# Fourier mixing: channel frequencies 0 to 128 computed, the others written as the same tiles at mirrored tokens

## The reference, cut to what matters

```python
FNET_GROUPS, FNET_GROUP_DIM = 4, 256
def fourier_mix(h, w_o, b_o):
    hg = h.astype(jnp.float32).reshape(bsz, t, FNET_GROUPS, FNET_GROUP_DIM)
    f = jnp.fft.fft2(hg, axes=(1, 3), norm='ortho').real
    return f.reshape(bsz, t, D_MODEL).astype(h.dtype) @ w_o + b_o

hx = rmsnorm(x, norm_g[i, 0]) * (1.0 + sc1x) + sh1x
x = x + g1x * fourier_mix(hx, fnet_wo[fi], fnet_bo[fi])
```

## Time and profile before

| | us |
|---|---|
| median of 3 runs | 4153.48 |
| lowest and highest | 4148.98, 4155.55 |
| the profiled execution's own time | 4151.23 |
| its span | 4149.3 |
| its mean granted TensorE clock | 0.956 |
| TensorE busy (share of the span) | 3711.9 (89%) |
| VectorE busy | 1350.4 (33%) |
| ScalarE busy | 1014.9 (24%) |

### The profile page before, as it was taken

The page is one execution under the profiler, slowest core; times in us unless marked ns, Lnnn a source line. Parts: engine busy times, 40 slices in busy tenths (PEclk is TensorE's granted clock), DMA queues, the critical chain, the costliest instruction groups (busy, mean ns, idle before and its releaser), DMA issues.

```text
span 4149.3 us, 63323 instructions
## 1 busy us (share of the span) xinstructions
PE 3711.9 (89%) x28370; PEld 2288.8 (55%) x28370; DVE 1350.4 (33%) x2376; ACT 1014.9 (24%) x1973; POOL 264.1 (6%) x240
## 2 busy tenths in 40 slices
PE   7998999999698969999768887779989998998998
PEld 3556443434355658888443332235548884656886
DVE  2123000000545047777430000025433332534243
ACT  3012111111232135554210000113323221423231
POOL 0000000000000034434100000000000000000000
PEclk9997999999888989999979999989999999999999
DMA  8345889896034154331519999911122322112230
GB/s 288 102 148 198 304 310 363 307 341 244 33 116 162 42 114 89 69 87 42 174 41 360 375 376 387 384 54 58 51 71 92 92 88 66 55 45 88 91 99 23
DMA packets 530414, 666.74 MB, mean 161 GB/s; under 512 B 156552, under 2 KB 299144, under 8 KB 530144
## 3 DMA queue, kind: packets, MB, share of 16 engines
q1 hardware_dynamic: 506352, 627.37, 44.6%
q10 hardware_dynamic: 19952, 22.81, 1.7%
q0 software_dynamic: 3840, 12.52, 0.8%
HBM read 631.18 MB, written 31.46 MB: 160 GB/s over the span
## 4 chain that ended last, share of the span: by engine, by line
PE 72%; DVE 10%; DMA 6%; SPq 4%; ACT 4%; POOL 2%; ACTq 1%; issue 1%; DVEq 0%; POOLq 0%
PE ps L620 11%; DMA ring<-in_moe_wu 5%; PE ps L625 4%; SPq L2652 4%; PE ps L483 3%; PE ps L813 3%; PE ps L2515 3%; PE ps L2516 3%; PE ps L2517 3%; PE ps L2531 3%; PE ps L2532 3%; PE ps L2530 3%; PE ps L786 3%; PE ps L2151 3%; PE ps L2257 3%; POOL ring L1323 2%
## 5 line engine op out<-in xcount | busy, mean ns | idle before, releaser
L620 PE MATMUL ps<-ring,H 128*64 128x512 f32 x2048 | 494.4, 602 | 52.4 <-DMA ring<-in_moe_wu 39.2
L620 PEld LDWEIGHTS ps<-ring,H 128*64 128x64 f32 x2048 | 146.9, 137 | 343.7 <-issue 253.9
L722 DVE TENSOR_TENSOR scr<-ps,scr 128x512 f32<-128x512 f32 x32 | 22.1, 691 | 965.2 <-PE ps L625 516.9
L620 PE MATMUL ps<-ring,scr 128*64 128x512 f32 x1024 | 248.3, 599 | 39.9 <-DMA ring<-in_moe_wd 38.5
L2515 PE MATMUL ps<-scr_rounded,ring_rounded 128*128 128x512 f32 x512 | 205.0, 400 | 23.0 <-ACT scr_rounded L2553 23.0
L2584 DVE TENSOR_TENSOR ring_rounded<-ring,scr_rounded 128x2048 fp32r<-128x2048 f32 x64 | 146.7, 2292 | 227.6 <-ACT scr_rounded L2550 227.6
L2516 PE MATMUL ps<-H_rounded,scr_rounded 128*128 128x512 f32 x512 | 204.8, 400 | 0.0
L2517 PE MATMUL ps<-scr_rounded 128*128 128x512 f32 x512 | 204.5, 399 | 0.0
L2532 PE MATMUL ps<-scr_rounded 128*128 128x512 f32 x512 | 202.6, 396 | 0.0
L2530 PE MATMUL ps<-scr_rounded,ring_rounded 128*128 128x512 f32 x512 | 202.0, 394 | 0.0
L2550 ACT ACTIVATE scr_rounded<-ring 128x2048 fp32r<-128x2048 f32 x64 | 122.1, 1908 | 257.7 <-PE ps L2532 246.4
(11 more groups left out here) (405 smaller groups left out, 6246.1 us busy)
## 6 DMA issues: line engine op xcount, KB each, us to landing
ring<-in_moe_wg SPq DMA_DIRECT2D x128, 1024.0 KB, 9.2
ring<-in_moe_wu SPq DMA_DIRECT2D x128, 1024.0 KB, 8.4
ring<-in_moe_wd SPq DMA_DIRECT2D x128, 1024.0 KB, 11.3
ring<-in_mlp_w SPq DMA_DIRECT2D x64, 1024.0 KB, 5.5
ring<-in_ada_w SPq DMA_DIRECT2D x48, 1024.0 KB, 8.0
ring<-in_w_in SPq DMA_DIRECT2D x14, 1024.0 KB, 5.2
ring<-in_w_out SPq DMA_DIRECT2D x8, 1024.0 KB, 5.2
st_kka<-scr ACTq DMA_DIRECT2D x16, 384.0 KB, 3.5
```

What stands on the lines that cost most here:

```text
L620: ins = pe.matmul(bx[64 * n:64 * n + 64, :], stat_x(k), w[:, k % 4, :], start=k == 0, stop=k == KT - 1)
```

## The change

The first table has 256 columns in place of 512: 129 cosines (frequencies 0 to 128) and 127 sines (frequencies 1 to 127). Two groups share a PSUM bank in the first transform. After it, VectorE and ScalarE put the columns of a bank in two places: in Z, frequencies 0 to 127 of the cosine and, from column 129 on, 1 to 127 of the sine (column 128, the sine of frequency 0, is set to zero once); and in ZH, a new tile, the cosine of frequency 128, one column per group at columns 0, 32, 64 and 96, the rest being zero.

The second transform makes one new tile per sequence from ZH (`fh`) and then, for each group, one tile of frequencies 0 to 127 instead of two tiles. Each such tile is written to H twice: as it is to tile 2g, and with its token columns reversed to tile 2g+1 (token 0 apart, by a copy of its own). Partition 0 of tile 2g+1, where frequency 128 belongs, is then overwritten from the `fh` tile. ScalarE takes groups 1 and 3, VectorE 0 and 2. The rows of the output weights are put in the matching order on the host. The modulation blocks in the first transform stand after the 1st, 2nd, 4th, 5th, 7th, 8th, 10th and 11th of its 12 banks; in the second, one after each group's tile.

```diff
-        DFT_C = S(12288, 2, 512)
+        DFT_C = S(12288, 2, 256)
...
-        Z = S(0, 6, 4, 512)
+        Z = S(0, 6, 4, 256)
+        ZH = S(6144, 6, P)
+        YH = [S(6912, TX), S(6912 + TX, TC)]
...
         def fnet_tensor(pe):
...
             for tt in range(6):
+                for gg in range(2):
+                    b = bank(pe, f"f1.{tt}.{gg}")
+                    for g in (2 * gg, 2 * gg + 1):
+                        o = 256 * (g % 2)
+                        for k in range(2):
...
+                            ins = pe.matmul(b[:, o:o + 256], H[:, 2 * g + k, tt * P:tt * P + P], DFT_C[:, k, :], start=k == 0, stop=k == 1)
+                    did(T_, ins.then_inc(tensor_done, 1), f"f1.{tt}.{gg}")
+                    if (2 * tt + gg) % 3 < 2:
+                        ada_tensor(pe, ADA_F1[0] + (2 * tt + gg) // 3 * 2 + (2 * tt + gg) % 3)
+            for s0, sn, tts in ((TX, TC, (4, 5)), (0, TX, (0, 1, 2, 3))):
...
+                for tt in tts:
+                    for gg in range(2):
+                        if later(pe, f"free.f1.{tt}.{gg}"):
+                            pe.wait_ge(*at(f"free.f1.{tt}.{gg}"))
+                b = bank(pe, f"fh.{s0}")
+                for n, tt in enumerate(tts):
+                    ins = pe.matmul(b[:, 0:sn], ZH[:, tt, :], table_of(n, 0), start=n == 0, stop=n == len(tts) - 1)
+                did(T_, ins.then_inc(tensor_done, 1), f"fh.{s0}")
                 for g in range(4):
...
+                    b = bank(pe, f"f2.{g}.{s0}")
                     for cs in range(2):
                         for n, tt in enumerate(tts):
...
+                            ins = pe.matmul(b[:, 0:sn], Z[:, tt, g, cs * P:cs * P + P], table_of(n, cs),
                                             start=cs == 0 and n == 0, stop=cs == 1 and n == len(tts) - 1)
...
+                    ada_tensor(pe, ADA_F2[0] + (0 if s0 else 4) + g)
+            linear_tensor(pe, "fo", "fwo", lambda k, s0, sn: H[:, k, s0:s0 + sn], SEGS, lambda k: f"fy.{k}",
                           between=lambda n: ada_tensor(pe, ADA_FO[0] + n))
...
         def fnet_scalar(act):
+            if later(act, "fz"):
+                act.wait_ge(*at("fz"))
             for tt in range(6):
+                for gg in range(2):
+                    if gg:
+                        t = tile(act, f"f1.{tt}.{gg}").rearrange("p (g c) -> p g c", c=256)
+                        for lo, hi in ((0, P), (P + 1, 2 * P)):
+                            did(A_, act.activation(Z[:, tt, 2:4, lo:hi], t[:, :, lo:hi], ACT.Copy).then_inc(scalar_done, 1))
+                        did(A_, act.activation(ZH[:, tt, 64:P].rearrange("p (g c) -> p g c", c=32)[:, :, 0:1], t[:, :, P:P + 1],
+                                               ACT.Copy).then_inc(scalar_done, 1), f"free.f1.{tt}.{gg}")
...
+            for s0, sn in (SEGS[1], SEGS[0]):
+                y = YH[1 if s0 else 0]
+                t = tile(act, f"fh.{s0}")
+                did(A_, act.activation(y, t[:, 0:sn], ACT.Copy).then_inc(scalar_done, 1), f"free.fh.{s0}")
                 for g in range(4):
                     if g % 2:
+                        t = tile(act, f"f2.{g}.{s0}")
+                        did(A_, act.activation(H[:, 2 * g + 1, s0 + 1:s0 + sn], t[:, sn - 1:0:-1], ACT.Copy).then_inc(scalar_done, 1))
+                        did(A_, act.activation(H[:, 2 * g + 1, s0:s0 + 1], t[:, 0:1], ACT.Copy).then_inc(scalar_done, 1))
+                        did(A_, act.activation(H[:, 2 * g, s0:s0 + sn], t[:, 0:sn], ACT.Copy).then_inc(scalar_done, 1), f"free.f2.{g}.{s0}")
+                        act.wait_ge(*own(act, A_))
+                        did(A_, act.activation(H[0:1, 2 * g + 1, s0:s0 + sn], y[32 * g:32 * g + 1, :], ACT.Copy).then_inc(scalar_done, 1))
...
+                    ada_scalar(act, ADA_F2[0] + (0 if s0 else 4) + g)
...
         def fnet_vector(dve):
+            did(V, dve.memset(Z[:, :, :, P:P + 1].rearrange("p t g c -> p (t g) c"), 0.0).then_inc(vector_done, 1))
+            did(V, dve.memset(ZH[:, :, :], 0.0).then_inc(vector_done, 1), "fz")
+            dve.wait_ge(*own(dve, V))
...
-    c["dftC"] = np.concatenate([cs, sn], 1)
+    c["dftC"] = np.concatenate([cs[:, 0:129], sn[:, 1:128]], 1)
...
+    n["fnet_wo"] = n["fnet_wo"][:, np.concatenate([mirrored[:, 0:128], mirrored[:, 128:256]], 1).reshape(-1), :]
```

More of the change, by code:

```diff
@@ L518, in fnet_tensor @@
             for tt in range(6):
-                for g in range(4):
[L520 to L527, removed]
@@ L528, in fnet_tensor @@
-            for s0, sn, tts in ((TX, TC, (4, 5)), (0, TX, (0, 1, 2, 3))):
-                for d in range(KT):
-                    b = bank(pe, f"f2.{d}.{s0}")
+                for gg in range(2):
[3 more added lines that the diff above has]
+                        for k in range(2):
+                            if later(pe, f"n0.h{2 * g + k}"):
+                                pe.wait_ge(*at(f"n0.h{2 * g + k}"))
+                            ins = pe.matmul(b[:, o:o + 256], H[:, 2 * g + k, tt * P:tt * P + P], DFT_C[:, k, :], start=k == 0, stop=k == 1)
+                    did(T_, ins.then_inc(tensor_done, 1), f"f1.{tt}.{gg}")
+                    if (2 * tt + gg) % 3 < 2:
+                        ada_tensor(pe, ADA_F1[0] + (2 * tt + gg) // 3 * 2 + (2 * tt + gg) % 3)
@@ new lines, in fnet_tensor, with table_of @@
+            for s0, sn, tts in ((TX, TC, (4, 5)), (0, TX, (0, 1, 2, 3))):
+                def table_of(n, cs):
+                    return DFT_T[:, n, cs * TX:cs * TX + TX] if s0 == 0 else DFT_TC[:, n, cs * TC:cs * TC + TC]
+                for tt in tts:
[6 more added lines that the diff above has]
+                did(T_, ins.then_inc(tensor_done, 1), f"fh.{s0}")
+                for g in range(4):
+                    b = bank(pe, f"f2.{g}.{s0}")
@@ L538, in fnet_tensor @@
                                             start=cs == 0 and n == 0, stop=cs == 1 and n == len(tts) - 1)
[L539 to L542, removed]
+                    did(T_, ins.then_inc(tensor_done, 1), f"f2.{g}.{s0}")
+                    ada_tensor(pe, ADA_F2[0] + (0 if s0 else 4) + g)
@@ L554, in fnet_scalar @@
+                        act.wait_ge(*own(act, A_))
+                        did(A_, act.activation(H[0:1, 2 * g + 1, s0:s0 + sn], y[32 * g:32 * g + 1, :], ACT.Copy).then_inc(scalar_done, 1))
+                        if s0 == 0:
+                            marks[f"fy.{2 * g}"] = marks[f"fy.{2 * g + 1}"] = (A_, count[A_])
+                    ada_scalar(act, ADA_F2[0] + (0 if s0 else 4) + g)
+            for b in range(*ADA_FO):
                 ada_scalar(act, b)
         def fnet_vector(dve):
+            did(V, dve.memset(Z[:, :, :, P:P + 1].rearrange("p t g c -> p (t g) c"), 0.0).then_inc(vector_done, 1))
@@ L557, in fnet_vector @@
+            did(V, dve.memset(ZH[:, :, :], 0.0).then_inc(vector_done, 1), "fz")
+            dve.wait_ge(*own(dve, V))
             for tt in range(6):
-                for g in range(0, 4, 2):
-                    t = tile(dve, f"f1.{tt}.{g}")
-                    did(V, dve.tensor_copy(Z[:, tt, g, :], t).then_inc(vector_done, 1), f"free.f1.{tt}.{g}")
-            for s0, sn in (SEGS[1], SEGS[0]):
-                for d in range(KT):
-                    t = tile(dve, f"f2.{d}.{s0}")
-                    did(V, dve.tensor_copy(H[:, d, s0:s0 + sn], t[:, 0:sn]).then_inc(vector_done, 1), f"free.f2.{d}.{s0}")
+                t = tile(dve, f"f1.{tt}.0").rearrange("p (g c) -> p g c", c=256)
+                for lo, hi in ((0, P), (P + 1, 2 * P)):
+                    did(V, dve.tensor_copy(Z[:, tt, 0:2, lo:hi], t[:, :, lo:hi]).then_inc(vector_done, 1))
+                did(V, dve.tensor_copy(ZH[:, tt, 0:64].rearrange("p (g c) -> p g c", c=32)[:, :, 0:1], t[:, :, P:P + 1]).then_inc(vector_done, 1),
+                    f"free.f1.{tt}.0")
@@ new lines, in fnet_vector @@
+            for s0, sn in (SEGS[1], SEGS[0]):
+                for g in (0, 2):
+                    t = tile(dve, f"f2.{g}.{s0}")
+                    did(V, dve.tensor_copy(H[:, 2 * g + 1, s0 + 1:s0 + sn], t[:, sn - 1:0:-1]).then_inc(vector_done, 1))
+                    did(V, dve.tensor_copy(H[:, 2 * g + 1, s0:s0 + 1], t[:, 0:1]).then_inc(vector_done, 1))
+                    did(V, dve.tensor_copy(H[:, 2 * g, s0:s0 + sn], t[:, 0:sn]).then_inc(vector_done, 1), f"free.f2.{g}.{s0}")
+                    if later(dve, f"free.fh.{s0}"):
+                        dve.wait_ge(*at(f"free.fh.{s0}"))
+                    dve.wait_ge(*own(dve, V))
+                    did(V, dve.tensor_copy(H[0:1, 2 * g + 1, s0:s0 + sn], YH[1 if s0 else 0][32 * g:32 * g + 1, :]).then_inc(vector_done, 1))
+                    if s0 == 0:
+                        marks[f"fy.{2 * g}"] = marks[f"fy.{2 * g + 1}"] = (V, count[V])
@@ L2911, in layout @@
         vecs[:, VEC[k]:VEC[k] + v.shape[1]] = v
+    mirrored = np.concatenate([np.arange(129), np.arange(255, 128, -1)]).reshape(1, 256) + 256 * np.arange(4).reshape(4, 1)
```

(1 more changed line is left out.)

3 lines of the change are left out of this document (2 added, 1 removed).

## The result

The changed kernel takes 4100.6 us (median of 4 runs, 4098.4 to 4105.7), the kernel before 4152.7 beside it. The ratio is 0.9877 with a 95% interval of 0.986 to 0.9894: 51 us, or 1.2%, faster. 4103 was forecast. The profiled execution took 4100.85 us with a span of 4098.8, 50.5 us less than the span before.

The account below looks back on a forecast made before the run. TensorE was taken to bound the Fourier stage, its time proportional to moving columns. Removing 50.3 us less a 1.1 us new wait gives 49.2 us, from 4151.2 to 4102.0 (4104.3 from the median); forecast 4103, range 4093 to 4115.

Parts of the forecast that it names:

- TensorE bounds the stage, and time goes by moving columns: Fourier stage: TensorE alone is the chain, 0.853 us per 512-column call, 0.427 per 256; 50.3 us removed.
- Modulation blocks unchanged: Both transforms: the 16 modulation blocks stay at 1.54 us each, in other places between the groups.
- Evacuations hidden: Both transforms: VectorE's and ScalarE's added copies and zero fills stay under TensorE's work, costing nothing; reversed copies at forward price.
- The wait with a new place: Start of second transform: TensorE waits for ScalarE's copies of the last first-transform tile, 1.1 us, bounds 0.6 and 2.
- What is late next, and the weights: Projection's start: ScalarE's last copies, about 2.2 us, hide under TensorE's 6.7; modulation weights arrive before they are wanted.
- The sum: Fourier stage: 50.3 us removed less 1.1 for the new wait, 49.2 us gained; stage end at 143.5 us.
- What comes behind moves forward whole: After the Fourier stage: the weight ring is full before the expert stage, so no lead is lost.
- rival D: Expert stage: weights arrive as late as before, transfers give the gain back, about 4150 us; 2% chance.
- A: First transform and context half: TensorE's clock stays low in the thinner work, 42 us extra, 4144 us; 3% chance.
- B: Whole Fourier stage: TensorE's clock stays low until the projection, 78 us extra, 4180 us, slower; 2% chance.
- C: Second transform: evacuation takes over through costly reversed reads, 4111 us at twenty times a forward one; 2% chance.

Follow-up runs that it names:

- run 1: Changed kernel with every group tile of the second transform multiplied twice into the same bank, evacuations as they are: 4133.6 us, ratio 0.9952.
- run 2: Kernel before, first transform whole, second computing only even frequency tiles, each copied forward to two tiles of H by VectorE: 4109.0 us, ratio 0.9891.
- Run 3: Changed kernel with the first transform's eight modulation blocks reordered so that the last bank has one behind it: 4095.8 us, ratio 0.9861.
- run 5: Changed kernel with five dense 512-column calls, result never read, in the norm stage behind the second modulation block: 4088.6 us, ratio 0.985.
- run 6: Changed kernel with a block behind the last bank, five dense calls in the norm's wait and nine before the router: 4085.3 us, ratio 0.9838.
- run 4: Changed kernel with two dense 512-column calls, result never read, between the second transform and the projection: 4100.8 us, ratio 0.9871.

## Why the prediction was right, step by step

**TensorE bounds the stage, and time goes by moving columns.** Right. The first transform kept 3.75 + 1.93 + 3 x 3.56 + 3 x 1.83 + 1.85 = 23.7 us (23.8 forecast), the context half 8.3 (8.3), the image half 31.3 (31.5). Runs 1 and 2 put the removed products back and took half of them away alone, and the stage moved by 35.0 and 33.6 us, 34.4 both times without the difference in the opening, where the count of columns gave 34.1.

**Modulation blocks unchanged.** Right but for the first one, which now comes 3.7 us into the stage instead of 7.4 and ran partly at the low pace, 1.32 us for its 16 records instead of 1.00. The clock had risen by the second bank.

**Evacuations hidden.** Right. VectorE's three copies of a token tile sum to 0.99 us (1 forecast). The reversed copies cost the forward price, which was the value taken. The one-partition copy was put at 0.57 us; it is 0.41 on VectorE and 0.63 on ScalarE. The zero fill of 768 columns took 0.70 (0.8).

**The wait with a new place.** Right, 0.89 us against 1.1. Run 3 shows it by moving a block behind the last bank. The forecast summed three durations; consecutive copies overlap a little in the trace, which is the difference (0.66 for two of 0.38).

**What is late next, and the weights.** Right. TensorE waits for no evacuation ahead of the projection and for no weights in the stage, and from the projection's start to its last block both kernels take 89.2 us.

**The sum.** 49.2 us forecast for the stage, 49.27 measured. So close a match of one trace each is in part luck, since the opening alone differs by over 1 us between traces of the same instructions (run 1). Its end was to be at 143.5 and is at 143.96, since the whole stage began 0.5 us later.

**"What comes behind moves forward whole."** True of the transfers, which is what the sentence argued from: the lead is 43.1 us at both ends of the expert stage, which runs near its transfer rate, so rival D is refuted. Not true of the clock. I had allowed 4 us, as an estimate, for what later restarts of TensorE may cost or give and said that they should mostly cancel. In the profiled run the norm stage cost 6.0 us, later stages returned 7.7 and the stage began 0.5 later, so the span fell by 1.2 us more than the stage. The total fits in part by luck, because two errors of that size met; each of them is larger than the 4 us allowed for all.

**The rivals.** A and B did not come: the clock reads 1.00 from 60 to 144 us. The rule cited beside A (the Trainium skill, page "TensorE: Matmul & The Clock Gate", section "A second HAM failure mode: psum-queue depth-cycling") did not come into play. It speaks of TensorE idling briefly between groups, and here TensorE is busy for 83.09 of the 84 us. Ahead of 60 us the opening ran at the low pace, before (7.36 us for six calls) as after (3.75 for four). But the mechanism named in A, modulation blocks running at 1.2 GHz pace after idle time, did come in the stage behind, for which the prediction had only its 4 us for all restarts, and took 6 us more than before. C falls by the row of the reversed copy, and D by the table of leads.

What stays open: where each later microsecond is gained or lost was read for two stretches only. From the router to the end the nine traces with the same work there differ by up to 10.5 us (3821.2 to 3831.7), and I tied this to the clock's stretches in the two shown, not in each. And it is open what decides, in the norm stage, whether the clock rises behind the norm's product (six traces) or not before the router (two).

## What to carry to other kernels

Where the chain is one engine without gaps, count the work unit that its durations are proportional to (here moving columns of fp32 calls), and take the price from a form that the trace already holds; that gave a 49 us change to within 1 us. Look for the last tile of a loop that loses the work standing behind it: its evacuation comes onto the path. And before crediting or blaming a stage for a few microseconds, follow the same instruction through both traces: an unchanged stage may differ by 6 us because TensorE idled ahead of it, and filling that idle time with dense calls brought more here than any order of the blocks.

## What the runs showed of the hardware

- Reading PSUM columns backwards costs no more than forwards: 511 reversed columns take 690 ns on VectorE and 596 on ScalarE, 512 forward ones 680 and 605.
- A copy of one partition costs what its columns cost, not less: 512 columns from SBUF take 414 ns on VectorE, where a copy of 128 partitions (L2768, SBUF to SBUF) takes 421, and 628 on ScalarE, where an activation on 128 partitions (L1390, SBUF to SBUF) takes 630.
- After idle time of 3.7 us in the norm stage TensorE ran at the low clock (blocks of 1.86 + 0.94 us in place of 1.00 + 0.54). Behind the same four dense records the clock rose at once in six traces and not before the router in two. With that idle time filled by five dense calls it did not fall (runs 5 and 6).
- Once high, the clock stayed high through five modulation blocks alone, 8.3 us from 243.86 us on (run 6, 1.00 from 230 to 261 us). In the router's 16-column records it fell some 5 us in (run 6).
- The clock column is no guide so early in a trace. Between 20 and 50 us it reads 1.00 before, after and in run 4, where a block takes 1.86 + 0.94 us and TensorE is busy for 23.5 us of the stretch; in the other seven traces it reads 0.78 to 0.86, and the same work is 19.8 to 21.8 us.
